# Loading queue of an MoE layer: the extra block's weights ahead of the last stage's, and two experts' weights behind one gathered row block instead of two

## What is computed

```python
u = rmsnorm(h, norm_ffn)
...
for e in range(N_EXPERTS):
    gu = jnp.einsum('bld,df->blf', u, w_gate_up[e])
    hid = jax.nn.silu(gu[..., :D_EXPERT]) * gu[..., D_EXPERT:]
    moe = moe + combine[..., e:e + 1] * jnp.einsum('blf,fd->bld', hid, w_down[e])
h = h + moe

u = rmsnorm(h, norm_ple)
gate = jax.nn.sigmoid(jnp.einsum('bld,de->ble', u, w_ple_gate))
h = h + gate * jnp.einsum('blp,pd->bld', p_l, w_ple_proj)
```

## Time and profile before

| | us |
|---|---|
| median of 3 runs | 850.83 |
| lowest and highest run | 850.77, 851.63 |
| the profiled execution, its own time | 849.0 |
| its span, first to last instruction | 847.2 |
| PE busy in the span | 822.9 (97%) |
| DVE, ACT, POOL busy | 385.5, 215.2, 152.6 |

### The profile page before, as it was taken

How to read it: one execution, slowest core, us unless ns; L and a number is a source line. 1 busy time by engine, 2 the same in 40 slices (tenths; PEclk the granted TensorE clock), 3 DMA queues, 4 the chain that set the end, 5 groups by cost and what they waited for, 6 DMA issues and landing times. The chain is left out here.

```text
span 847.2 us, 13448 instructions
## 1 busy us (share of the span) xinstructions
PE 822.9 (97%) x5462; PEld 519.9 (61%) x5462; DVE 385.5 (46%) x857; ACT 215.2 (25%) x464; POOL 152.6 (18%) x184
## 2 busy tenths in 40 slices
PE   8999999999999999999999999999999999979996
PEld 4546777888889987777777775455343333334452
DVE  3223556676646522664852559546441111105543
ACT  3202153258223311131001101123031111114554
POOL 0234420014054133300220052001000000004000
PEclk9999999999999999999999999999999999989999
DMA  9420344402020110522252024005899999966111
GB/s 361 193 99 25 133 150 163 155 1 108 1 101 4 45 58 13 198 72 99 100 198 100 1 100 178 25 26 209 352 415 417 427 421 420 406 279 198 50 38 50
DMA packets 19197, 135.31 MB, mean 160 GB/s; under 512 B 2496, under 2 KB 3136, under 8 KB 11712
## 3 DMA queue, kind: packets, MB, share of 16 engines
q1 hardware_dynamic: 11888, 104.33, 31.2%
q0 software_dynamic: 4896, 24.48, 7.8%
q10 hardware_dynamic: 2352, 5.64, 2.0%
HBM read 119.01 MB, written 19.63 MB: 164 GB/s over the span
## 5 line engine op out<-in xcount | busy, mean ns | idle before, releaser
L765 PE MATMUL pair<-mem 128*128 128x288 f32 x640 | 158.9, 408 | 0.0
L765 PEld LDWEIGHTS pair<-mem 128*128 128x128 f32 x640 | 120.3, 190 | 35.6 <-ACT mem L1381 2.1
L935 PE MATMUL single<-mem 128*128 128x288 f32 x448 | 110.0, 407 | 0.3
L935 PEld LDWEIGHTS single<-mem 128*128 128x128 f32 x448 | 84.7, 190 | 25.7 <-issue 1.6
L1275 PE MATMUL single<-mem 128*32 128x512 f32 x768 | 85.1, 594 | 1.1 <-DVE mem L2304 0.9
L1381 ACT ACTIVATE mem<-single 128x256 f32<-128x256 f32 (+5 forms) x111 | 45.6, 421 | 134.7 <-PE single L1181 48.7
L1381 ACT ACTIVATE mem<-pair 128x512 f32<-128x512 f32 (+5 forms) x77 | 33.5, 485 | 156.7 <-PE pair L765 63.0
L1360 PE MATMUL pair<-mem 128*128 128x512 f32 (+1 forms) x192 | 63.3, 524 | 0.0
L1275 PEld LDWEIGHTS single<-mem 128*32 128x32 f32 x768 | 24.0, 110 | 52.7 <-issue 51.6
L2297 DVE SCALAR_TENSOR_TENSOR mem<-single,mem 128x256 f32<-128x256 f32 x12 | 5.8, 484 | 104.3 <-PE single L1275 91.4
L1172 PE MATMUL pair<-mem 128*128 128x512 f32 x112 | 51.0, 601 | 0.0
(11 more groups left out here) (407 smaller groups left out, 1135.2 us busy)
## 6 DMA issues: line engine op xcount, KB each, us to landing
mem<-in_w_gu SPq DMA_DIRECT2D x17, 2048.0 KB, 14.8
mem<-in_w_down SPq DMA_DIRECT2D x17, 1024.0 KB, 14.9
y_slots<-mem SPq DMA_DIRECT2D x12, 512.0 KB, 11.1
y_slots<-in_zeros POOLq DMA_DIRECT2D x8, 512.0 KB, 7.8
mem<-in_w_ga SPq DMA_DIRECT2D x2, 2048.0 KB, 7.6
mem<-in_w_gb SPq DMA_DIRECT2D x2, 2048.0 KB, 7.6
mem<-in_w_wo SPq DMA_DIRECT2D x2, 2048.0 KB, 7.7
mem<-in_w_pg SPq DMA_DIRECT2D x2, 2048.0 KB, 14.1
```

What stands on the lines that cost most here:

```text
L765: last = nc.tensor.matmul(pb[:, hf, 0:HALF], w(k), rhs[:, k, hf * HALF:(hf + 1) * HALF], start=(k == 0), stop=(k == kk - 1))
L935: last = nc.tensor.matmul(single[plan.buf[s]][:, 0:HALF], lhs[:, k, :], rhs[:, k, :], start=(k == 0 and j in (0, 1, 3, 4)), stop=(k == 3), ...
```

## The change

Three things move on the queues, and one transfer is dropped. `w_proj` and `w_pg0` leave the phase loop of SP and are issued behind the extra block's weights, with `pT` between them, which moves from POOL's queue to SP's. SP waits for `xg0` only ahead of experts 2 and 3. `pT4` is dropped: tile 4 is read from `pT`. Without the wait for the last transpose, POOL reaches its extra-block loop right after its twelfth gather. PE waits for both `w_proj` and `pT` on one semaphore.

```diff
                 if e == 2:
                     sp.wait_ge(sem("xg0"), 16)
-                    sp.wait_ge(sem("xg1"), 16)
                 load_gu(e)
...
-                if p == NPH - 2:
-                    sp.dma_start(view(BLK, CHUNK_W), a["w_pg0"]).then_inc(sem("w_pg"), 16)
...
-                if p == NPH - 3:
-                    sp.dma_start(w_proj.rearrange("p k c -> p (k c)"), a["w_proj"]).then_inc(sem("w_proj"), 16)
...
                     sp.dma_start(w_dn_flat[0], a["w_down"][bass.ds(e * P, P), :]).then_inc(sem("ov_w"), 16)
+            sp.dma_start(w_proj.rearrange("p k c -> p (k c)"), a["w_proj"]).then_inc(sem("ld_p"), 16)
+            sp.wait_ge(sem("xT_mm"), NPH)
+            sp.dma_start(pT, a["pT"]).then_inc(sem("ld_p"), 16)
+            sp.dma_start(view(BLK, CHUNK_W), a["w_pg0"]).then_inc(sem("w_pg"), 16)
             store(NPH - 2)
...
-            pe.wait_ge(sem("ld_p"), 16)
-            pe.wait_ge(sem("w_proj"), 16)
+            pe.wait_ge(sem("ld_p"), 32)
...
-                if t == 4:
-                    pe.wait_ge(sem("ld_p"), 32)
...
-                            last = nc.tensor.matmul(pair[t % 2][rows, hf, cols], pT[:, k, t * P:t * P + n] if t < 4 else pT4[:, k, :],
+                            last = nc.tensor.matmul(pair[t % 2][rows, hf, cols], pT[:, k, t * P:t * P + n],
...
-            pool.wait_ge(sem("xT_mm"), NPH)
-            pool.dma_start(pT, a["pT"]).then_inc(sem("ld_p"), 16)
             pool.wait_ge(sem("ov_ready"), 3)
...
-            pool.wait_ge(sem("ld_p"), 16)
-            pool.dma_start(pT4, a["pT"][:, :, 4 * P:TOK]).then_inc(sem("ld_p"), 16)
```

More of the change, by code:

```diff
@@ L517, in build @@
         pT = view(OR, 2, TOK)
-        pT4 = view(BLK + 17408, 2, 64)
         lg = sb("lg", [P, NT, 20])
```

## The result

The changed kernel is slower: 853.17 us against 850.77, medians of 17 runs each; the ratio is 1.0030 with a 95% interval of 1.0020 to 1.0041, so 1.7 to 3.5 us. In a second series the ratio was 1.0035 (1.0020 to 1.0051). I had forecast 848.2.

What follows compares the result with a forecast made beforehand. PE, busy 97% of the span, was taken as the bound, losing time to late extra-block weights and slow clock. L1344 3.8 us earlier plus 1.2 us clock cost gave -2.6 us, from 850.83 to 848.2; range 846.3 to 851.7.

Steps and rivals of the forecast that it cites:

- the old bound: Before L1303, PE waited about 3.6 us for the extra block's weights alone, which stood late in SP's line of bytes.
- the first half of the sum: Extra block on PE: weights land by 742.5, L1303 starts 3.9 us earlier and takes 1.75, products start near 749.8.
- the step on the stores and POOL: End of SP's line: last store lands at 758.7, POOL's first gather of results goes out near 758.8, 2.2 us earlier.
- the path's main term: PE's first L1344, behind combine 0, starts near 767.0, 3.8 us earlier; the rest of the last stage follows.
- Issue of the extra block's weights: On SP's queue, issued at 732.3 instead of 732.60, earlier by the 0.27 us won at 705.46.
- The line behind them: SP's queue behind the gate and up part: 7.93 MB at 0.424 MB per us, 18.7 us, last store landing at 758.7.
- ACT's stores: The extra block's four stores, issued up to 752.2 into full engines, land about 3.5 us after the last issue, bounds 1.5 and 9.9.
- From landing to gather: On POOL: ready at 756.5, so the first gather goes out near 758.8, right behind the store landing at 758.7.
- The third rival: ACT's extra-block stores fall behind in full engines, landing at 762.1, gather at 762.9: +2.0 us, 852.8; chance 0.11.
- the second: Gain eaten: SP's queue gap near 730 costs more, last store lands at 760 to 761: -0.3 us, 850.5; chance 0.22.
- The clock cost: PE idles 1.6 to 3.3 us ahead of L1344; slow clock then costs 1.2 us of a range 0 to 1.7.
- the first rival: Full gain: clock stays up or the line runs faster, L1344 starts with PE hardly idle: -3.8 to -4.9 us, 846.5; chance 0.15.

Runs made afterwards that it cites:

- SP's stores first: The changed kernel with w_pg0 and w_pg1 issued behind the stores of phases 10 and 11; ratio 1.0051 to the kernel before.
- the filler: The changed kernel with six matmuls of unread result in PE's wait before the first u3 transpose; ratio 1.0007 to the kernel before, median 849.46 us.
- the rest of the change: The changed kernel with SP's waits for both xg0 and xg1 put back; ratio 1.0032 to the kernel before.

## Why the prediction was wrong, step by step

**What held.** The reading of the old bound was right, and so was the first half of the sum. The extra block's weights landed 7.6 us after their issue. PE started their matmuls 3.7 us earlier (forecast 3.9), they took 1.95 us (forecast 1.75), and the products started 5.1 us earlier (forecast 5.5) and took 14.0 us (forecast 13.9 without a slow stretch). `pT` and `w_proj` were there in time. `pT4` was worth 1.1 us on POOL.

**What failed is the step on the stores and POOL.** I had the first gather of results 2.2 us earlier than before; counted from G it went out 1.33 us later. So the path's main term fell too: L1344 was to start 3.8 us earlier and started 0.7 us earlier. The gather's error of 3.5 us has three terms:

- *Issue of the extra block's weights, 1.4 us.* I let SP issue them 0.27 us earlier than before, at G + 142.0. They went out at 143.4, although the store ahead of them went out on time. SP began its read of the number of extra blocks 0.4 us later behind that store than before, and the read took 0.86 us longer:

```profile
L714 SPq TENSOR_LOAD <-ovi x1: 1333/1333/1333, 732.4 to 732.4; - x1
```

  Before it was 469 ns, right behind the store's issue.
- *The line behind them, 1.5 us.* From their landing to SP's last store I had 7.93 MB at 424 GB/s, 18.7 us. It took 20.2. The engines moved 407 GB/s in this stretch and not the 424 of the middle phases, which is half of the error; the other half is 0.3 MB that I had not put in the line, such as ACT's stores and what `norm_final` had moved by then.
- *From landing to gather, 0.7 us.* I let POOL start 0.1 us after the last landing. The chain shows 0.8.

**ACT's stores were mis-sized too.** I took 3.5 us of bounds 1.5 and 9.9; the last needed 7.9, and 9.1 with SP's stores first. By their landing at 761.9 and 0.8 us for the loop's end they alone would have held the gather at G + 171, by estimate. Scaling the 1.5 us by the ratio of two gathers was the mistake: for these small stores the time does not grow in proportion; the last ended within 0.2 us of `w_pg1` in the changed kernel and in the one with the stores first. The third rival named this mechanism, at a chance of 0.11, and the second named the gap near 730, at 0.22; both were at work. That the third's 852.8 us is near the 853.17 measured is in part luck: it had the first u3 transpose 0.3 us later than before, and from G it was 0.7 us earlier, while its 1.7 us of slow clock was short by 0.2 to 0.9. The rule of the Trainium skill that I cited (page "DMA: Bandwidth & Descriptors", section "Queues, rings and completion order") on queues taking turns did not protect them. The same section of the Trainium skill also says that the semaphore increment of a transfer lands only after every earlier write of that DMA engine, across its queues. The runs agree with a completion that comes with the line, 7.9 and 9.1 us against 1.5 in quiet engines, but no run here tells that apart from plain sharing of the engines.

**The clock cost was mis-sized by 0.7 us or more.** I had a wait of 1.6 to 3.3 us and 1.2 us of cost. The wait was 5.95 us and the cost 1.9, shown by the filler, and 2.6 in the second profile of the same kernel.

**The sum with measured terms.** First u3 transpose 0.7 us earlier from G (180.5 to 179.8), slow clock 1.9 us: 1.2 us slower, and the spans from G say 1.3. The medians say 2.4. The rest lies in how single executions differ. Three profiles have the old order of the loads (before, without the second wait, without `pT4`): from G they took 256.9, 255.1 and 256.7 us, and two of them contain the second slow stretch. Three have the new order (the changed kernel twice, and the rest of the change): 258.15, 258.9 and 258.7. The means differ by 2.3 us, close to the medians. Three profiles a side are few, so this split is likely and not proven.

**The step I did not take.** I wrote that the queue "is nearly empty from about 729.5 until the weights start at 733, and all of it has to be made up", and priced it by adding up bytes. I did not ask what would have filled it. `w_pg0` had, and leaving it there turned the loss into a gain.

One figure in the first rival was not fit for its use: by the name of its section in the Trainium skill, the formula of 2.0 us and 436 GB/s is one for GpSimd's transfers, and I applied it to SP's. It put the last store at G + 167.0, and the store landed at G + 171.2.

## What to carry to other kernels

Putting an urgent transfer ahead of less urgent ones did not pay here while one of them had been filling time in which the queue's engine waits for something else, and it paid once that one stayed. So look at what SP waits for in front of the urgent issue, and leave in that place whatever can already go. Small stores at the end of a stage must be priced by the load that they meet, not by their size, and the whole line should be followed to the wait behind it, since in five of the kernels here freeing one transfer only moved the wait. Read how long a step takes from more than one execution where the clock is involved.

## What the runs showed of the hardware that was not expected

- A 32 KB store on ACT's queue landed in 1.5 us in quiet engines and in 7.9 to 9.1 us beside a full SP queue. In one kernel, with the line still running, ACT needed 5.14 us just to issue four of them, instead of 1.9.
- SP's read of one number from SBUF took 1333 ns in the changed kernel and 469 in the one before. It took 1312 to 1333 ns in all seven profiles of kernels that read it after the phases and load `w_proj` only behind it, the one with `w_pg0` kept in front among them, and 464 to 477 in the other six. Why is open.
- PE's wait of 5.95 us was followed by a granted clock of 0.50, at a cost of 1.9 us (2.6 in a second profile, behind 5.92 us); a wait of 1.21 us (`w_pg0` kept) was not, and six unread matmuls in the long wait prevented it.
- The first four gathers of 128 rows of results took 4.2 to 6.0 us with SP's line at its end, and the first three 11.3 to 14.2 us with three loads of SP just issued.
